# Scale's four modulation units as products on TensorE, the row norm ahead of them, the norm's copies in 256 columns

## The chip, the cores and the metric

The kernel runs on one core of a Trainium2 chip. The metric is the device time of one execution in microseconds; lower is better. Five engines work side by side and meet only at semaphores: TensorE (PE, matmuls; its weight loads are shown apart as PEld), VectorE (DVE), ScalarE (ACT), GpSimd (POOL) and SyncE (SP), which issues most of the DMAs.

## The reference

Two blocks of layers run one after the other over 256 tokens of width 1024, all in float32. The first block has two hybrid layers, the second two layers with a mixer and a mixture of experts. The change touches the beginning of the first layer of the first block:

```
mod = (c_act @ w_ada + b_ada)[:, None, :]          # 1024 -> 6 * 1024
sh1, sc1, g1, sh2, sc2, g2 = jnp.split(mod, 6, axis=-1)
h = rmsnorm(x, norm1_w) * (1 + sc1) + sh1
u = h @ w_in
```

c_act is silu(c), one row of 1024 numbers. So shift (sh1) and scale (sc1) are two vectors of 1024, each the product of one row with a 1024 x 1024 matrix, and nothing of the layer's products can start without both.

## The kernel before

The tokens are two row tiles of 128; the width is 8 chunks of 128. Each large product is made of three: weights and activations are split into a high half (fp32r, written by ScalarE as a copy) and a low half (the difference, written by VectorE), and TensorE adds high x high, high x low and low x high (`product`, L2148). Weights come in groups of 1 MB through a ring of three raw slots; SyncE loads the next group into a slot when VectorE has read it (L710, semaphores raw_read). The halves of a group lie in whi and wlo, three groups each.

The modulation is computed in units of 1 MB: unit n covers two chunks of 128 input rows for one of the six vectors. Units 0 to 3 are shift's, 4 to 7 scale's, 8 is the first unit of the gate's. Units 0 to 2 lie in the raw slots; units 3 to 8 lie in raw_deep, which is the same memory as the halves: unit 3 where the first group's high half will go, unit 6 where its low half will go (`early`, L620). SyncE issues them in the order unit 0, x, units 1 to 7, then two groups of w_in, then unit 8 and some constants (L687 to L703).

`early_ada` (L1286) is VectorE's work on one unit: for each of its two chunks, a row of 1024 is multiplied by one number per partition and added to an accumulator [128 x 1024]. After four units `sum_mod` (L2131) lets TensorE sum the accumulator over the partitions: for each of 8 column blocks one matmul with the block as stationary side and one column of ones as the moving side. `take_mod` (L1325) adds the bias columns, `norm_columns` (L1339) makes the columns by which the norm scales.

Each engine runs its instructions in the order in which the program writes them. VectorE at the start of layer 0 (L1556 to L1583): c_act, units 0 and 1, the transposed parameter columns (pcol), unit 2, the mean squares and inverse roots of the two row tiles (`mean_square`, `rsqrt`), units 3 to 7, shift and scale, norm_columns, the low half of group 0, then the norm's copies. ScalarE (L882 to L893): the squares, roots and row scaling of both tiles, the high half of group 0 once both accumulators are done (L888), the high halves of the copies, the high half of group 1. TensorE (L2204 to L2218): turns the scaled rows tile by tile (`turn_tile`), the two sums, then product 0 for row tile 0 and for row tile 1, and product 1.

The norm's copies (`modulated`, L1361) go from PSUM to the buffer ft, which has two places: four instructions of 128 columns for each of four quarters (row tile, half of the width). `high_tile` on ScalarE and `low_tile` on VectorE make the halves of a quarter. In the other places of the kernel a PSUM bank holds two chunks of 256 tokens, and `turn`, `high` and `low` handle a bank.

Of the kernel before, what the change touches and what calls it, by code (L numbers as in the profile page):

```python
# [29 lines left out]
ALU = mybir.AluOpType  # L30
# [3 lines left out]
P = 128  # L34
T = 256
D = 1024
KD = D // P
NT = T // P
# [31 lines left out]
ADA = 4  # L70
# [177 lines left out]
def program(nc, A, out):  # L248
    with ExitStack() as top:
# [27 lines left out]
        ft = sb("ft", [P, 2, 2 * T])  # L277
# [342 lines left out]
        def early(n):  # L620

            part = raw[:, n] if n < RAW else raw_deep[:, n - RAW]
            return parts_of(part, 2, D)
# [196 lines left out]
        def _(act):  # L820
# [13 lines left out]
            for l in range(LAYERS):  # L834
# [20 lines left out]
                def high_tile(f, t, h):  # L855

                    act.wait_ge(*ft_ready.at(l, ft_index(f) + 1))
                    act.activation(tile_part(xt_hi, t, h), chunks_of_tile(ft[:, f % 2, :]), ACT.Copy).then_inc(ft_hi.sem, 1)
# [23 lines left out]
                if l == 0:  # L882
                    for t in range(NT):
                        square(t)
                    for t in range(NT):
                        root(NORM1 + t, t, t + 1)
                        scale_rows(NORM1, t)
                    act.wait_ge(*acc_done.at(0, 2))  # L888
                    split(0)
                    for t in range(NT):  # L890
                        for h in range(2):
                            high_tile(X_NORM1 + 2 * t + h, t, h)
                    split(1)  # L893
                else:

                    act.wait_ge(*x_final.at(l - 1, 5))
                    square(0)
                    root(NORM1, 0, 1)
                    scale_rows(NORM1, 0)
                    split(1)  # L900
                    act.wait_ge(*x_final.at(l, 0))
                    square(1)
                    for h in range(2):
                        high_tile(X_NORM1 + h, 0, h)
                    root(NORM1 + 1, 1, 2)
                    scale_rows(NORM1, 1)
                    for h in range(2):
                        high_tile(X_NORM1 + 2 + h, 1, h)
# [289 lines left out]
        def _(dve):  # L1198
# [46 lines left out]
            for l in range(LAYERS):  # L1245
# [40 lines left out]
                def early_ada(n):  # L1286

                    vec, i = divmod(n, ADA)

                    dve.wait_ge(early_in[n], 16)  # L1290
                    if i == 0:

                        dve.wait_ge(*acc_read.at(0, vec - 1))
                    w, a = early(n), acc[:, vec % 2, :]
                    for k in range(2):
                        c = cact[:, 2 * i + k:2 * i + k + 1]
                        if i == 0 and k == 0:
                            ins = dve.tensor_scalar(a, w[:, k, :], c, None, ALU.mult)
                        else:
                            ins = dve.scalar_tensor_tensor(out=a, in0=w[:, k, :], scalar=c, in1=a, op0=ALU.mult, op1=ALU.add)  # L1300
                        if k == 0:
                            lk(ins)
                    ins.then_inc(early_read, 1)
                    dve.wait_ge(early_read, n + 1)
                    if n < RAW:
                        dve.sem_inc(raw_read[n].sem, 1)
                    if i == ADA - 1:
                        dve.sem_inc(acc_done.sem, 1)
# [16 lines left out]
                def take_mod(vec, l=l):  # L1325

                    dve.wait_ge(*acc_read.at(l, vec + 1))
                    if vec in (2, 5):
                        i = vec // 3

                        dve.wait_ge(*grow_in.at(l, 32))
                        b = MOD_BANK[vec]
                        dve.tensor_tensor(grow[:, i, :], mp[:, b:b + 2, :].rearrange("p a n -> p (a n)"), grow[:, i, :], ALU.add).then_inc(mod_taken.sem, 1)
                    else:
                        c = MOD_COL[vec]
                        src = gp[:, 0, vec, 0:KD] if l == 0 and vec < 2 else mp[:, MOD_BANK[vec], c:c + KD]
                        dve.tensor_tensor(modc[:, vec, :], src, pcol[:, l, KD * vec:KD * (vec + 1)], ALU.add).then_inc(mod_taken.sem, 1)

                def norm_columns(i, vec, l=l):  # L1339

# [215 lines left out]
                if l == 0:  # L1556
                    dve.wait_ge(csig_ready, 1)
                    lk(dve.tensor_tensor(cact[:, :], mp[:, 2, 0:KD], csig[:, :], ALU.mult))
                    early_ada(0)
                    early_ada(1)  # L1560
                    dve.wait_ge(params_t, LAYERS)
                    for i in range(LAYERS):
                        dve.tensor_copy(pcol[:, i, :], mp[:, i, 0:PC_ROWS]).then_inc(params_ready, 1)
                    dve.wait_ge(params_ready, LAYERS)
                    early_ada(2)
                    for t in range(NT):
                        mean_square(0, t)
                    for t in range(NT):
                        rsqrt(NORM1 + t, t, t + 1)
                    for n in range(3, 2 * ADA):  # L1570
                        early_ada(n)
                    take_mod(0)
                    take_mod(1)
                    norm_columns(0, 0)
                    split(0)
                    modulated(X_NORM1, 0, 0, 0, 0)
                    for t, h in ((0, 1), (1, 0), (1, 1)):
                        modulated(X_NORM1, 0, 0, t, h)
                        low_tile(X_NORM1, *((0, 0), (0, 1), (1, 0))[2 * t + h - 1])
                    low_tile(X_NORM1, 1, 1)  # L1580
                    split(1)
                    early_ada(2 * ADA)
                    dve.wait_ge(params_in, PARAMS)  # L1583
                else:
                    norm_tail(X_NORM1, 0, 0, NORM1, 0, lambda: split(1))
# [532 lines left out]
        def _(pe):  # L2118
# [25 lines left out]
                mm.then_inc(acc_read.sem, 1)  # L2144


            for l in range(LAYERS):
                def product(s, tiles=range(NT)):  # L2148

# [52 lines left out]
                    pe.wait_ge(*mod_taken.at(l, 2))  # L2202

                if l == 0:  # L2204
                    for t in range(NT):
                        pe.wait_ge(*xn_ready.at(l, t + 1))
                        turn_tile(t)
                    pe.wait_ge(zeroed, 2)
                    sum_mod(0, 0)
                    sum_mod(1, 0)  # L2210
                    pe.wait_ge(*mod_taken.at(0, 2))
                if l == 0:
                    pe.wait_ge(*ft_lo.at(l, X_NORM1 + 1))
                    product(0, (0,))
                    pe.wait_ge(*ft_lo.at(l, X_NORM1 + 3))
                    product(0, (1,))
                    pe.wait_ge(*ft_lo.at(l, X_NORM1 + 4))
                    product(1)  # L2218
                else:
                    begin(0, X_NORM1, 0)  # L2220
                poolcur = poolw[:, l, :, :]
# [492 lines left out]
```

## Time and profile before

| | |
|---|---|
| median of three runs | 1791.11 us (1787.89 to 1794.01) |
| the profiled execution's own time | 1795.38 us |
| its span | 1793.6 us |
| TensorE busy | 1581.0 us, 88% |
| VectorE busy | 938.0 us, 52% |
| ScalarE busy | 620.4 us, 35% |
| DMA | 427.65 MB, 238 GB/s in the mean |

The span is from the first to the last recorded instruction. Busy shares are means over stages with different limits; what an edit is worth is read from the waits of its own stage. In a row of a timeline the first number is the start in us, the second the time from the start of the first to the end of the last of the instructions that it merges; in brackets stands the idle time before them and what ended it.

### The profile page before, as it was taken

To read this page: it belongs to the slowest core of one execution; us is meant where nothing else is said; L and a number is where in the kernel's file an instruction comes from. 1 tells how busy PE (TensorE), PEld (TensorE's weight loads), DVE (VectorE), ACT (ScalarE), POOL (GpSimd) and SP (SyncE) were. 2 spreads that over 40 slices of the span, in tenths; PEclk is the share of its full clock that TensorE was granted. 3 is DMA by queue.
4 is the path that set the end of the run, shared out by engine and by line. 5 is a ranking of instruction groups with operands and counts; after the bars stand their busy time and mean duration, and the time that the engine had idled before them with its cause. 6 is when DMAs were issued, how large, how long until landed. Compare 5 with 4: busy or idle time off the path is not lost.

```text
span 1793.6 us, 18858 instructions
## 1 busy us (share of the span) xinstructions
PE 1581.0 (88%) x7463; PEld 1088.6 (61%) x7463; DVE 938.0 (52%) x1402; ACT 620.4 (35%) x881; POOL 49.8 (3%) x66
## 2 busy tenths in 40 slices
PE   2799988999889998899979995999996996799985
PEld 2687767888768776788868874333334875433331
DVE  4897667765478666764556665110006675311102
ACT  2354444433345444443425651111114472111111
POOL 2000000000000000000020200000000010000000
PEclk9999999999989998999989897999998998899998
DMA  9576534876466543575646425999994516599994
GB/s 338 197 236 213 185 119 168 307 244 242 164 216 241 200 164 128 172 235 169 219 128 204 129 83 200 377 409 409 409 400 144 167 48 247 200 409 409 409 409 190
DMA packets 149963, 427.65 MB, mean 238 GB/s; under 512 B 8104, under 2 KB 16544, under 8 KB 149872
## 3 DMA queue, kind: packets, MB, share of 16 engines
q1 hardware_dynamic: 146192, 417.43, 63.6%
q0 software_dynamic: 3456, 8.87, 1.8%
q8 instruction: 64, 1.05, 0.2%
q14 instruction: 27, 0.22, 0.0%
q10 hardware_dynamic: 224, 0.07, 0.0%
HBM read 425.30 MB, written 1.05 MB: 238 GB/s over the span
## 4 chain that ended last, share of the span: by engine, by line
PE 43%; DVE 7%; SPq 6%; DMA 3%; issue 1%; ACT 1%; DVEq 0%
PE gp L2164 11%; PE gp L2553 9%; PE gp L2372 9%; SPq L734 6%; PE gp L2572 4%; PE mp L2593 2%; DMA raw_more<-in_exp_w_up 2%; PE gp L2538 2%; PE mp L2427 1%; PE mp L2426 1%; PE mp L2391 1%; DVE stats L1706 1%; PE mp L2415 1%; PE mp L2435 1%; DMA raw<-in_w_in 1%
## 5 line engine op out<-in xcount | busy, mean ns | idle before, releaser
L1315 DVE TENSOR_TENSOR wlo<-raw,whi 128x2048 fp32r<-128x2048 f32 (+1 forms) x132 | 289.5, 2194 | 206.5 <-ACT whi L842 205.2
L2164 PE MATMUL gp<-whi,xt_hi 128*128 128x512 f32 (+1 forms) x800 | 320.1, 400 | 31.9 <-DVE xt_lo L1376 20.5
L842 ACT ACTIVATE whi<-raw 128x2048 fp32r<-128x2048 f32 (+1 forms) x132 | 242.2, 1835 | 300.0 <-PE gp L2164 188.1
L2164 PE MATMUL gp<-wlo,xt_hi 128*128 128x512 f32 (+1 forms) x800 | 312.9, 391 | 0.0
L2164 PE MATMUL gp<-whi,xt_lo 128*128 128x512 f32 (+1 forms) x800 | 312.5, 391 | 0.0
L2164 PEld LDWEIGHTS gp<-whi,xt_hi 128*128 128x128 f32 x800 | 155.4, 194 | 72.2 <-DVE xt_lo L1376 15.9
L2164 PEld LDWEIGHTS gp<-whi,xt_lo 128*128 128x128 f32 x800 | 155.4, 194 | 31.4
L2164 PEld LDWEIGHTS gp<-wlo,xt_hi 128*128 128x128 f32 x800 | 155.7, 195 | 30.0 <-issue 1.0
L2031 DVE TENSOR_SCALAR pr<-slots,key,dg 128x128 f32<-128x128 f32 x64 | 19.3, 344 | 260.5 <-PE gp L2583 260.5
L2372 PE MATMUL gp<-whi,xt_hi 128*128 128x512 f32 (+1 forms) x224 | 86.2, 385 | 6.0 <-DVE xt_lo L1751 3.1
L1225 DVE SCALAR_TENSOR_TENSOR acc<-raw,cact,acc 128x1024 f32<-128x1024 f32 x69 | 88.5, 1282 | 2.5 <-DMA raw<-in_w_ada 1.1
L2045 DVE TENSOR_TENSOR pr<-pr,gp 64x512 f32<-64x512 f32 x32 | 21.7, 679 | 123.2 <-ACT pr L1145 123.2
L2372 PE MATMUL gp<-whi,xt_lo 128*128 128x512 f32 (+1 forms) x224 | 84.6, 378 | 0.0
L2372 PE MATMUL gp<-wlo,xt_hi 128*128 128x512 f32 (+1 forms) x224 | 84.6, 378 | 0.0
L1242 DVE TENSOR_TENSOR wlo<-raw,whi 128x2048 fp32r<-128x2048 f32 (+3 forms) x32 | 59.5, 1859 | 34.1 <-ACT whi L1018 32.8
L1139 ACT ACTIVATE cgc<-gp 128x256 f32<-128x256 f32 x32 | 12.3, 384 | 185.7 <-PE gp L2583 185.7
L2164 PE MATMUL gp<-whi,at_hi 128*128 128x512 f32 x176 | 69.9, 397 | 4.3 <-DVE at_lo L1414 4.3
L2164 PE MATMUL gp<-wlo,at_hi 128*128 128x512 f32 x176 | 69.2, 393 | 0.0
L2164 PE MATMUL gp<-whi,at_lo 128*128 128x512 f32 x176 | 69.1, 392 | 0.0
L2572 PE MATMUL gp<-raw_deep,pr 128*64 128x512 f32 x288 | 65.4, 596 | 1.5 <-ACT pr L1140 1.5
L2553 PE MATMUL gp<-raw_deep,xg_second 128*64 128x512 f32 x256 | 61.6, 626 | 5.7 <-DMA raw_deep<-in_exp_w_up 5.7
L1018 ACT ACTIVATE whi<-raw 128x2048 fp32r<-128x2048 f32 (+3 forms) x36 | 57.4, 1601 | 25.4 <-PE gp L2372 13.4
(390 smaller groups left out, 2356.0 us busy)
## 6 DMA issues: line engine op xcount, KB each, us to landing
raw<-in_w_in SPq DMA_DIRECT2D x60, 1024.0 KB, 5.5
raw<-in_w_ada SPq DMA_DIRECT2D x42, 1024.0 KB, 5.5
raw_deep<-in_exp_w_down SPq DMA_DIRECT2D x36, 1024.0 KB, 16.9
raw_deep<-in_exp_w_gate SPq DMA_DIRECT2D x30, 1024.0 KB, 14.4
raw_deep<-in_exp_w_up SPq DMA_DIRECT2D x30, 1024.0 KB, 16.8
raw<-in_w_gate SPq DMA_DIRECT2D x20, 1024.0 KB, 5.1
raw<-in_w_up SPq DMA_DIRECT2D x20, 1024.0 KB, 5.1
raw<-in_w_down SPq DMA_DIRECT2D x20, 1024.0 KB, 5.0
```

The source lines that it names most:

```text
L734: sp.dma_start(parts_of(part, units, cols), src).then_inc(there.sem, 16)
L842: act.activation(slot(whi, s % SPLIT, units, cols), slot(raw, g % RAW, units, cols), ACT.Copy).then_inc(hi_done.sem, 1)
L1018: act.activation(slot(whi, s % SPLIT, units, cols), parts_of(part, units, cols), ACT.Copy).then_inc(hi_done.sem, 1)
L1225: ins = dve.scalar_tensor_tensor(out=a, in0=w[:, k, :], scalar=c, in1=a, op0=ALU.mult, op1=ALU.add)
L1242: dve.tensor_tensor(slot(wlo, s % SPLIT, units, cols), parts_of(part, units, cols), slot(whi, s % SPLIT, units, cols).bitcast(F32), ALU.su ...
L1315: dve.tensor_tensor(slot(wlo, s % SPLIT, units, cols), slot(raw, g % RAW, units, cols), slot(whi, s % SPLIT, units, cols).bitcast(F32), AL ...
L2164: mm = pe.matmul(gp[:, q % 2, t, 0:wide], a[:, chunk, ts], w[:, unit, c0:c0 + wide], start=first and n == 0 and m == 0, stop=last and n == ...
L2372: mm = pe.matmul(gp[:, q % 2, t, 0:cols], a[:, chunk0 + unit, ts], w[:, unit, :], start=first and unit == 0 and m == 0, stop=last and unit ...
L2538: mm = pe.matmul(bank, h[:, t, P * c:P * (c + 1)], pick[:, t, :], start=t == 0 and h is h_hi, stop=t == 1 and h is h_lo)
L2553: mm = pe.matmul(bank[columns, :], a[:, chunk0 + c, column0:column0 + CAP], w[:, c, :], start=first and c == 0, stop=last and c == 3)
L2572: mm = pe.matmul(bank_y[CAP * n:CAP * (n + 1), :], ag[:, CAP * chunk:CAP * (chunk + 1)], w[:, c, COLS * n:COLS * (n + 1)], start=chunk == ...
L2593: mm = pe.matmul(mp[:, 2 * t + half, :], back[rows, P * t:P * (t + 1)], yx[rows, :], start=e == 0, stop=e == NE - 1)
```

## The change

Four things change, all in layer 0 of the first block.

1. VectorE takes units 0 to 3 only, and the parameter columns and both row norms come right behind unit 0, ahead of unit 1.
2. Units 4 to 7 become matmuls on TensorE (`unit_product`): a 128 x 128 block of the unit is the stationary side, the chunk's column of c_act the moving side, and the results add up in 8 columns of a PSUM bank, which start from scale's bias columns by a product with the identity. VectorE then copies these columns instead of adding the bias. TensorE sums the shift's accumulator ahead of the last unit. ScalarE's first split waits for TensorE's last unit (acc_read) instead of VectorE's (acc_done), because it overwrites what TensorE reads.
3. TensorE turns both row tiles together, bank by bank, and products 0 and 1 are each made for both tiles at once.
4. The norm's copies are made bank by bank, two instructions of 256 columns each, in an order in which two banks go ahead of VectorE's first split.

```diff
@@ ScalarE
-                    act.wait_ge(*acc_done.at(0, 2))
+                    act.wait_ge(*acc_read.at(0, 2))
                     split(0)
-                    for t in range(NT):
-                        for h in range(2):
-                            high_tile(X_NORM1 + 2 * t + h, t, h)
+                    for b in range(4):
+                        high(X_NORM1 + b, xt_hi[:, 2 * b:2 * b + 2, :])
                     split(1)
@@ early_ada
-                    dve.wait_ge(early_read, n + 1)
+                    dve.wait_ge(early_read, n + 1 if n < ADA else n + 1 - ADA)
@@ take_mod
-                        dve.tensor_tensor(modc[:, vec, :], src, pcol[:, l, KD * vec:KD * (vec + 1)], ALU.add).then_inc(mod_taken.sem, 1)
+                        if l == 0 and vec == 1:
+                            dve.tensor_copy(modc[:, vec, :], src).then_inc(mod_taken.sem, 1)
+                        else:
+                            dve.tensor_tensor(modc[:, vec, :], src, pcol[:, l, KD * vec:KD * (vec + 1)], ALU.add).then_inc(mod_taken.sem, 1)
@@ VectorE, layer 0
                     early_ada(0)
-                    early_ada(1)
                     dve.wait_ge(params_t, LAYERS)
                     for i in range(LAYERS):
                         dve.tensor_copy(pcol[:, i, :], mp[:, i, 0:PC_ROWS]).then_inc(params_ready, 1)
                     dve.wait_ge(params_ready, LAYERS)
-                    early_ada(2)
                     for t in range(NT):
                         mean_square(0, t)
                     for t in range(NT):
                         rsqrt(NORM1 + t, t, t + 1)
-                    for n in range(3, 2 * ADA):
+                    for n in range(1, ADA):
                         early_ada(n)
                     take_mod(0)
                     take_mod(1)
                     norm_columns(0, 0)
+
+                    def normed(b):
+                        f = X_NORM1 + b
+                        bank_done(f)
+                        for k in range(2):
+                            c = 2 * b + k
+                            ins = dve.tensor_scalar(ft[:, f % 2, T * k:T * (k + 1)], mp[:, b, T * k:T * (k + 1)],
+                                                    scol[:, 0, c:c + 1], modc[:, 0, c:c + 1], ALU.mult, ALU.add)
+                            if k == 0:
+                                lk(ins)
+                        ins.then_inc(ft_ready.sem, 1)
+
+                    def low_bank(b):
+                        low(X_NORM1 + b, xt_hi[:, 2 * b:2 * b + 2, :], xt_lo[:, 2 * b:2 * b + 2, :])
+
+                    normed(0)
+                    normed(1)
+                    low_bank(0)
                     split(0)
-                    modulated(X_NORM1, 0, 0, 0, 0)
-                    for t, h in ((0, 1), (1, 0), (1, 1)):
-                        modulated(X_NORM1, 0, 0, t, h)
-                        low_tile(X_NORM1, *((0, 0), (0, 1), (1, 0))[2 * t + h - 1])
-                    low_tile(X_NORM1, 1, 1)
+                    low_bank(1)
+                    normed(2)
+                    normed(3)
+                    low_bank(2)
+                    low_bank(3)
                     split(1)
                     early_ada(2 * ADA)
@@ TensorE
+            def unit_product(vec, i):
+
+                pe.wait_ge(early_in[ADA * vec + i], 16)
+                w = early(ADA * vec + i)
+                if i == 0:
+
+                    pe.matmul(gp[:, 0, vec, 0:KD], ident[:, :], pcol[:, 0, KD * vec:KD * (vec + 1)], start=True, stop=False)
+                for k in range(2):
+                    j = 2 * i + k
+                    for c in range(KD):
+                        mm = pe.matmul(gp[:, 0, vec, c:c + 1], w[:, k, P * c:P * (c + 1)], cact[:, j:j + 1],
+                                       start=False, stop=j == KD - 1 and c == KD - 1)
+                if i == ADA - 1:
+                    mm.then_inc(acc_read.sem, 1)
@@ TensorE, layer 0
-                    for t in range(NT):
-                        pe.wait_ge(*xn_ready.at(l, t + 1))
-                        turn_tile(t)
+                    pe.wait_ge(*xn_ready.at(l, 2))
+                    for b in range(4):
+                        turn(b, xn2, 2 * P * b).then_inc(tr_done.sem, 1)
                     pe.wait_ge(zeroed, 2)
-                    sum_mod(0, 0)
-                    sum_mod(1, 0)
+                    for i in range(ADA):
+                        if i == ADA - 1:
+                            sum_mod(0, 0)
+                        unit_product(1, i)
+                    pe.sem_inc(acc_done.sem, 1)
                     pe.wait_ge(*mod_taken.at(0, 2))
                 if l == 0:
-                    pe.wait_ge(*ft_lo.at(l, X_NORM1 + 1))
-                    product(0, (0,))
-                    pe.wait_ge(*ft_lo.at(l, X_NORM1 + 3))
-                    product(0, (1,))
-                    pe.wait_ge(*ft_lo.at(l, X_NORM1 + 4))
-                    product(1)
+                    for s in range(2):
+                        pe.wait_ge(*ft_lo.at(l, X_NORM1 + 2 * s + 2))
+                        product(s)
```

## Rows read from the trace of the kernel before

**Rows 1.** The page: the span and TensorE's busy time, share and instructions.
```profile
span 1793.6 us, 18858 instructions
PE 1581.0 (88%) x7463; PEld 1088.6 (61%) x7463; DVE 938.0 (52%) x1402; ACT 620.4 (35%) x881; POOL 49.8 (3%) x66
```

**Rows 2.** Timeline of SyncE's queue: the issues of units 4 and 7.
```profile
4.98 0.50 SPq L685 DMA_DIRECT2D raw_deep<-in_w_ada  x1
...
13.34 7.05 SPq L685 DMA_DIRECT2D raw_deep<-in_w_ada  x1
```

**Rows 3.** DMA issues: the same two, KB, then us from issue to landing.
```profile
raw_deep<-in_w_ada SPq DMA_DIRECT2D x1, 1024.0 KB, 24.4
...
raw_deep<-in_w_ada SPq DMA_DIRECT2D x1, 1024.0 KB, 23.8
```

**Rows 4.** Timeline of all engines, 14 to 31 us: units and row norm.
```profile
14.36 1.28 ACT L863 ACT_TABLE_LOAD   x1
...
19.25 2.60 DVE L1300 SCALAR_TENSOR_TENSOR acc<-raw,cact,acc 128x1024 f32<-128x1024 f32 x2 [9.42 <-DMA raw<-in_w_ada]
...
27.62 1.15 ACT L871 ACTIVATE xn<-x,rr 128x1024 f32<-128x1024 f32 x1 [1.00 <-DVE rr L1354]
...
28.91 1.94 PE L2173 MATMUL mp<-ident,xn 128*128 128x128 f32 x8 [16.04 <-ACT xn L871]
```

**Rows 5.** Timeline of all engines, 32 to 46.3 us: the two sums over partitions.
```profile
32.82 3.41 PE L2143 MATMUL gp<-ones,acc 128*128 128x1 f32 x16
...
42.65 1.91 ACT L842 ACTIVATE whi<-raw 128x2048 fp32r<-128x2048 f32 x1 [11.64 <-DVEq L1308]
...
42.67 3.57 PE L2143 MATMUL gp<-ones,acc 128*128 128x1 f32 x16 [6.43 <-DVEq L1308]
...
46.28 0.17 DVE L1337 TENSOR_TENSOR modc<-gp,pcol 128x8 f32<-128x8 f32 x1 [3.41 <-PE gp L2143]
```

**Rows 6.** Timeline of all engines, 48 to 77 us: copies, splits, first products.
```profile
48.89 3.40 DVE L1366 TENSOR_SCALAR ft<-mp,scol,modc 128x128 f32<-128x128 f32 x8
50.67 0.63 ACT L858 ACTIVATE xt_hi<-ft 128x512 fp32r<-128x512 f32 x1 [6.11 <-DVE ft L1366]
52.21 0.68 DVE L1376 TENSOR_TENSOR xt_lo<-ft,xt_hi 128x512 fp32r<-128x512 f32 x1
...
52.99 0.76 PE L2164 MATMUL gp<-whi,xt_hi 128*128 128x512 f32 x1 [6.75 <-DVE xt_lo L1376]
...
59.71 2.29 DVE L1315 TENSOR_TENSOR wlo<-raw,whi 128x2048 fp32r<-128x2048 f32 x1 [1.11 <-ACT whi L842]
...
62.15 0.47 PE L2164 MATMUL gp<-whi,xt_hi 128*128 128x512 f32 x1 [0.86 <-DVE wlo L1315]
...
74.05 2.28 DVE L1315 TENSOR_TENSOR wlo<-raw,whi 128x2048 fp32r<-128x2048 f32 x1
76.25 1.28 DVE L1225 SCALAR_TENSOR_TENSOR acc<-raw,cact,acc 128x1024 f32<-128x1024 f32 x1
```

**Rows 7.** Line 2143, the sums: ns min/median/max, first and last start.
```profile
L2143 PEld LDWEIGHTS mp<-ones,acc x96: 188/192/338, 213.5 to 662.9; 128*128 128x128 f32 x96
...
L2143 PEld LDWEIGHTS gp<-ones,acc x32: 287/333/337, 32.6 to 45.8; 128*128 128x128 f32 x32
L2143 PE MATMUL gp<-ones,acc x32: 213/352/372, 32.8 to 45.9; 128*128 128x1 f32 x32
```

**Rows 8.** Stretches: length, busy us and instructions by engine, granted clock, DMA share, GB/s.
```profile
213.60:215.60 2.00, 2.00 (x21) 2.00 (x20) 1.93 (x4) 0.00 (x0) 0.00 (x0) 0.99 1.05 390
215.60:218.40 2.80, 2.80 (x15) 2.80 (x15) 0.06 (x1) 0.00 (x0) 0.00 (x0) 0.50 0.98 333
53.00:58.60 5.60, 5.60 (x13) 4.38 (x14) 5.17 (x11) 1.99 (x3) 0.00 (x0) 1.00 0.07 28
58.60:61.30 2.70, 2.68 (x12) 1.88 (x10) 1.59 (x1) 2.70 (x2) 0.00 (x0) 1.00 0.00 0
```

**Rows 9.** Line 1623: a copy of 256 columns from PSUM, ns min/median/max.
```profile
L1623 DVE TENSOR_SCALAR ft<-mp,pcol x4: 483/484/486, 220.7 to 665.9; 128x256 f32<-128x256 f32 x4
```

**Rows 10.** SyncE's waits from 62 us on: total us, times, longest.
```profile
SPq L693 <- DVE wlo L1315: 690.9, 124, 19.4
SPq L734 <- DVE wlo L1242: 268.3, 32, 48.2
```

## The prediction

> **What bounds the kernel now.** I read the page's first part, then the start of the run as a timeline, then the DMA issues, then the waits behind the start. TensorE is busy 88% of the span [rows 1], so most of the run is a chain of products on TensorE, fed by splits that ScalarE and VectorE make. The page's chain of waits is followed back only to 675 us, so the stage that changes has to be read from the timeline.
>
> At the start the chain is this. SyncE issues the loads of eight modulation units in a row, 0 to 3 for shift and 4 to 7 for scale. They land one behind the other: unit 4 at 4.98 + 24.4 = 29.4 us, unit 7 at 13.34 + 23.8 = 37.1 us [rows 2, 3]. VectorE takes them one at a time, 2.60 us for two accumulations [rows 4], and is done with unit 7 at about 42.6. TensorE then sums the second accumulator over the partitions: 16 matmuls in 3.57 us, to 46.24 [rows 5]. VectorE forms the columns, splits the first weights, writes the norm's copies, and the first product starts at 52.99 [rows 6]. From there VectorE is the one that ends last: the second split starts at 59.71, then a leftover unit, a split, another unit and the rotary angles follow without a gap to the split of 74.05 [rows 6]; TensorE waits for it. So what counts is how much the VectorE operation of 59.71 moves. The path to it is: columns known (46.24), plus 13.47 us.
>
> **Part 1, row norm ahead.** The parameter columns and the two row norms go ahead of unit 1. ScalarE's squares are ready at 14.3 and its table for the root is loaded from 14.36 for 1.28 us [rows 4], so the first root comes at 15.7, the five short VectorE steps after it end at 16.8, ScalarE's scaling of 1.15 us [rows 4] ends at 18.0, the second root and steps end at 19.1 and the second scaling at 20.2. VectorE is free at 19.1, just before unit 1 lands (it starts on it at 19.25 now [rows 4]), so this costs nothing there: the DMA's landing hides it. The turns of both row tiles, 8 in 1.94 us [rows 4], take 16 x 0.24 = 3.9 us and end at 24.2 instead of 33.0. Nothing waited for them before 46.68, so this gains nothing by itself: it moves them out of TensorE's way, which now has other work from 29.4 on.
>
> **Part 2, VectorE's half.** Units 4 to 7 leave VectorE: 4 x 2 accumulations, some 10.1 us. The landings are (37.1 - 29.4) / 3 = 2.6 us apart, so unit 3 lands at about 26.8 and VectorE has finished it at 29.5. From then VectorE idles until the columns come. The loads behind it are not touched: the two raw slots are released by units 0 and 1, at the same times as before.
>
> **Part 3, TensorE's half, the term that decides.** One unit is 2 chunks x 8 columns = 16 matmuls with a 128x128 block of weights in f32 as the stationary side and a single moving column. The trace has this operation: the sum over partitions is 8 such matmuls, and appears as 16 instructions with 16 weight loads [rows 5, 7]. So each matmul is two instructions. Sixteen of them took 3.57 us with the last one lasting 0.35 [rows 7], hence (3.57 - 0.35) / 15 = 0.2147 us from one to the next. It is the weight load that is paid, for a single column, and there is no saving from having only one column. Counted out: 2 for the bias columns (identity by parameter columns), 4 x 32 = 128 for the units, and 16 for the first accumulator's sum, which stands between units 6 and 7. Together 146 instructions x 0.2147 = 31.35 us. They start when unit 4 lands, at 29.45 us, and no later unit is late: one lands every 2.6 us and takes 6.9 us to multiply. The last ends at 29.45 + 31.35 + 0.14 (the tail of the last one) = 60.95 us. In the kernel before the same point was 46.24: 14.7 us later. VectorE needed 2.60 us for a unit, TensorE needs 6.9.
>
> Why the slow price: the loads of these sums last 333 ns at the start and 192 ns in the median later on [rows 7]. In the later place the first 2 us held 21 instructions at a granted clock of 0.99, and the next 2.8 us held 15 at 0.50 [rows 8]; so the engine had its 2.4 GHz level from the dense products before, and fell to 1.2 GHz in the middle of a run of one-column matmuls, which did not keep it. At the start the printed clock is 1.00, but the spacing of the first dense products says 1.2 GHz: 13 of 512 columns in 5.6 us, then 12 in 2.7 us [rows 8]. They rose only after 5.6 us of dense work; the 7.5 us of turns and sums before (28.9 to 36.4) had not raised it, since the sum at 42.67 is still at 0.21 [rows 5]. From both sides: the price is 0.107 where the engine stays at full clock (half of 0.2147, and about the 21 in 2 us), and 0.333 if no load overlaps the matmul before it. I take 0.2147: same shape, same level, same DMA load (the first sum ran while the queues were full).
>
> The Trainium skill, "TensorE: Matmul & The Clock Gate", section "LDWEIGHTS (loading the stationary operand)", gives a load as the column count over 1.2 GHz, 107 ns for 128 columns, whatever the rows. By that rule 146 loads would be an estimated 15.6 us and TensorE would nearly keep up with the landings; the row's 0.215 is twice it, and the measurement decides the sum.
>
> **Part 4, behind the columns.** Call E the end of the last unit's product. ScalarE waited for the accumulators before (42.65) and splits the first weights beside TensorE's second sum [rows 5]; now its buffer is free only at E, because the units lie where the halves go. Split from E to E + 1.9 [rows 5], and the high copy behind it. VectorE: copy of the scale columns and the norm columns to E + 0.44; two copies of 256 columns, 4 x 0.484 [rows 9], to E + 2.4. The high copy of bank 0 ends at E + 2.55 (0.63 each), the low one (0.68 [rows 6]) at E + 3.25, the split (2.29) at E + 5.5, the second low at E + 6.15. The first product starts at E + 6.2 = 67.2, against 52.99. Copies 2 and 3 end at E + 8.15, their lows at E + 9.6; ScalarE's second split begins at E + 8.8 behind its last high copy and takes 1.9, so VectorE's second split starts at E + 10.8. Before it was 13.47 behind: 16 copies of 128 columns, 8 of them in 3.40 us [rows 6], have become 8 of 0.484, and the tile-wise order with its waits has gone. This part gives back 2.7 us. Product 0, now in one piece, runs from 67.2 at the low level first: 5.6 + 11 x 0.226 = 8.1 us, to 75.3; product 1 follows to 80.8 and product 2 to 86.3.
>
> **The sum.** VectorE's second split: 60.95 + 10.8 = 71.75 against 59.71, so +12.0 us. Behind it VectorE's row is the same and unbroken, so the split of 74.05 moves to 86.1 and ends at 88.4, after product 2 (86.3): VectorE still ends last there, and all of the 12.0 goes on. The loads of the following slots start when VectorE has read a slot (SyncE's longest wait is that one, 690.9 us in 124 times [rows 10]), so the transfers move by the same amount and nothing runs ahead of it. Own time 1795.38 (span 1793.6) + 12.0 = 1807.4. The runs' median is 1791.11, 4.3 us below the profiled one, so the forecast is 1791.1 + 12.0 = 1803.1 us.
>
> **The rivals.**
> A, the other side: a unit costs TensorE half. For it: at the full level the same matmul goes at 0.107 [rows 8]. The place is the run from 29.45; the units would take 3.4 us each and E comes at 29.45 + 146 x 0.107 = 45.1, which is 1.1 before today's; with Part 4 the second split starts at 55.9, 3.8 us earlier: 1787.3, faster. It decides below a price of 0.13: E + 10.8 equals 59.71 at E = 48.9, which leaves 19.3 us for 146 instructions. Against it: three runs of this shape show the low level. The Trainium skill's rule on the weight load, above, would end here too.
> B, slower at the start but given back later: 1791 to 1794. For it: SyncE waits a lot, and a later stage that was bound by transfers could hide the delay. Against: the wait of SyncE is for VectorE's reads, so no transfer runs ahead [rows 10]; the mechanism needs a load that starts by itself.
> C, dearer: the loads don't overlap, since here each brings a new 1 MB of weights that a transfer has just written: 146 x 0.333 = 48.6, E = 78.1, +29.2: 1820. Against: the same matmul overlapped at the start with the queues full.
> D, the clock rises part of the way: after some of the 31 us of steady work TensorE gets 2.4 GHz. Half the run at 0.107 gives E = 53, +4 us: 1795. For it: the longest unbroken run of such matmuls in [rows 8] is 4.8 us, and 31 us of them are not shown. Against: those fell, none rose.
>
> **How the numbers follow.** The forecast has 0.77, A 0.07, B 0.05, C 0.04, D 0.07. A kernel like this can't be told from no change within 0.3%, 5.4 us. Faster: A less a part of its noise, 0.07. Same: B, most of D: 0.08. Slower: 0.85. The range: the forecast's own is 1803 plus or minus 5 (the three runs before lie 6 us apart, and the terms of Part 4 are good to 1 us); down to D it is 1797, up 1809. That leaves out A, B and C, 0.16 with the edges.
>
> **What would show it.** In the profile after: a unit's 32 instructions in about 6.9 us; loads of 333 ns; the last unit's end at 61; ScalarE's first split at 61 instead of 42.65; the first product at 67; VectorE's second split at 71.8; DVE idle from 29.5 to 54. Units with loads of 0.19 would prove A or D; a first product at 67 and a span under 1800 would prove B.

## The result, and the profile after

| | before | after |
|---|---|---|
| median of six runs | 1793.83 us | 1805.45 us (1803.1 to 1809.11) |
| profiled execution, span | 1793.6 us | 1807.3 us |

The ratio is 1.0069, with a 95% interval of 1.0053 to 1.0085: slower by 9.5 to 15.3 us, clear of what a measurement can tell from no change. The forecast was +12.0 us. The forecast's level, 1803.1, is 2.3 below the measured one. It was added to a median of the kernel before over three runs, 1791.11; over six runs that median is 1793.83, 2.7 higher, so the difference is the better test of the two.

The page after: span, then busy time, share and instructions by engine; it answers to [rows 1]. TensorE has 114 instructions more (130 for the units and the bias, 16 fewer for the sum that is gone) and is busy 27 us longer; VectorE is busy 12 us less.

```profile
span 1807.3 us, 19064 instructions
PE 1608.1 (89%) x7577; PEld 1114.4 (62%) x7577; DVE 926.0 (51%) x1386; ACT 620.3 (34%) x881; POOL 49.7 (3%) x66
```

The changed stage as a timeline, all engines (start us, us, engine, line, operation; in brackets the idle time before and what ended it), answering to [rows 4 to 6]. "Turns" are the 128 x 128 transposes of the scaled rows, "the columns" are shift and scale laid out over the partitions:

```profile
20.87 3.65 PE L2228 MATMUL mp<-ident,xn 128*128 128x128 f32 x16 [7.89 <-ACT xn L871]
...
26.96 2.61 DVE L1299 SCALAR_TENSOR_TENSOR acc<-raw_deep,cact,acc 128x1024 f32<-128x1024 f32 x2 [1.02 <-DMA raw_deep<-in_w_ada]
...
29.62 0.57 PE L2171 MATMUL gp<-pcol,ident 128*128 128x8 f32 x2 [5.11 <-DMA raw_deep<-in_w_ada]
...
30.04 20.62 PE L2175 MATMUL gp<-cact,raw_deep 128*128 128x1 f32 x96
...
50.52 3.55 PE L2161 MATMUL gp<-ones,acc 128*128 128x1 f32 x16
...
53.94 6.97 PE L2175 MATMUL gp<-cact,raw_deep 128*128 128x1 f32 x32
54.11 0.17 DVE L1339 TENSOR_TENSOR modc<-gp,pcol 128x8 f32<-128x8 f32 x1 [24.55 <-PE gp L2161]
60.94 0.17 DVE L1337 COPY modc<-gp 128x8 f32<-128x8 f32 x1 [6.66 <-PE gp L2175]
60.94 1.91 ACT L842 ACTIVATE whi<-raw 128x2048 fp32r<-128x2048 f32 x1 [40.21 <-PE gp L2175]
...
67.00 0.76 PE L2197 MATMUL gp<-whi,xt_hi 128*128 128x512 f32 x1 [6.10 <-DVE xt_lo L1398]
...
71.46 2.29 DVE L1314 TENSOR_TENSOR wlo<-raw,whi 128x2048 fp32r<-128x2048 f32 x1 [1.11 <-ACT whi L842]
...
85.79 2.28 DVE L1314 TENSOR_TENSOR wlo<-raw,whi 128x2048 fp32r<-128x2048 f32 x1
...
88.13 0.50 PE L2197 MATMUL gp<-whi,xt_hi 128*128 128x512 f32 x1 [2.02 <-DVE wlo L1314]
```

The reader is to see three things. TensorE is busy from 29.62 to 60.91, 31.28 of the 31.30 us in the stretch below. VectorE stands idle for 24.55 and then 6.66 us, waiting for it, and ScalarE for 40.21. And the second split starts at 71.46, where it started at 59.71: 11.75 us later, and the split of 74.05 [rows 6], that of weight group 3, at 85.79: 11.74 later; nothing was given back on the way.

The units' instructions (ns min/median/max, first and last start), then three stretches with their length, busy us and instructions by engine, granted clock, DMA share and GB/s: the whole stretch, and two pieces of 6.9 us, about a unit each. An instruction that overlaps an edge of a stretch is counted in it.

```profile
L2175 PEld LDWEIGHTS gp<-cact,raw_deep x128: 333/333/333, 30.0 to 60.5; 128*128 128x128 f32 x128
L2175 PE MATMUL gp<-cact,raw_deep x128: 352/352/352, 30.0 to 60.5; 128*128 128x1 f32 x128
```

```profile
29.60:60.90 31.30, 31.28 (x146) 31.21 (x146) 0.17 (x1) 0.00 (x0) 0.00 (x0) 0.50 0.53 198
...
36.40:43.30 6.90, 6.90 (x34) 6.90 (x34) 0.00 (x0) 0.00 (x0) 0.00 (x0) 0.50 1.05 390
...
53.70:60.60 6.90, 6.90 (x34) 6.90 (x34) 0.17 (x1) 0.00 (x0) 0.00 (x0) 0.50 0.00 0
```

146 instructions in 31.3 us at a granted clock of 0.50, the 1.2 GHz level: 0.2145 each. The count is the same, 34 in 6.9 us, with the transfers at 390 GB/s and with none at all, so the transfers don't set this price. Here the clock column says the level itself; at the start of the kernel before it printed 1.00, and only the spacing and the loads of 333 ns showed the level [rows 7, 8].

### The profile page after: what moved, and what is told of

Same layout as the page of the kernel before. It is cut to its first block, busy times and chain, and to the rows that moved or that the text cites. A ratio compares the mean times of both kernels' runs of the same rounds, so it can differ in the third digit from the quotient of the medians.

```text
span 1807.3 us, 19064 instructions
## 1 busy us (share of the span) xinstructions
PE 1608.1 (89%) x7577; PEld 1114.4 (62%) x7577; DVE 926.0 (51%) x1386; ACT 620.3 (34%) x881; POOL 49.7 (3%) x66
## 4 chain that ended last, share of the span: by engine, by line
PE 43%; DVE 7%; SPq 6%; DMA 3%; issue 1%; ACT 1%; DVEq 0%
PE gp L2197 11%; PE gp L2586 9%; PE gp L2405 9%; SPq L734 6%; PE gp L2605 4%; PE mp L2626 2%; DMA raw_more<-in_exp_w_up 2%; PE gp L2571 2%; PE mp L2460 1%; PE mp L2459 1%; PE mp L2424 1%; DVE stats L1724 1%; PE mp L2468 1%; PE mp L2448 1%; DMA raw<-in_w_in 1%
## 5 line engine op out<-in xcount | busy, mean ns | idle before, releaser
L2197 PEld LDWEIGHTS gp<-whi,xt_lo 128*128 128x128 f32 x800 | 154.8, 193 | 31.3
L2197 PEld LDWEIGHTS gp<-wlo,xt_hi 128*128 128x128 f32 x800 | 155.4, 194 | 29.8 <-issue 1.0
```

Source lines behind the costliest of these rows:

```text
L2197: mm = pe.matmul(gp[:, q % 2, t, 0:wide], a[:, chunk, ts], w[:, unit, c0:c0 + wide], start=first and n == 0 and m == 0, stop=last and n == ...
```

## The experiments

**All units back on VectorE** (norm ahead and wide copies stay; the addition of scale's bias and the semaphores go back with the units, which the diff below leaves out).

```diff
-                    for n in range(1, ADA):
+                    for n in range(1, 2 * ADA):
                         early_ada(n)
...
-                    for i in range(ADA):
-                        if i == ADA - 1:
-                            sum_mod(0, 0)
-                        unit_product(1, i)
-                    pe.sem_inc(acc_done.sem, 1)
+                    sum_mod(0, 0)
+                    sum_mod(1, 0)
```

> The changed kernel with one part undone: all eight units go back to VectorE (row norm ahead and copies in 256 columns stay). My theory: the 146 one-column instructions on TensorE are the whole loss, and the other two parts gain. VectorE follows the landings and ends unit 7 at 37.1 + 2.7 = 39.9 us, TensorE's sum takes 3.5, so the columns come at 43.5; the second split 10.6 us behind, at 54.1 instead of 59.7: 5.6 us faster than the kernel before, ratio 0.997. Rival: the new order of VectorE and ScalarE behind the columns costs something of its own (ScalarE's first split now delays the high copies, product 0 waits for both tiles): then the second split would come at 59 or later and the kernel would be no faster than before.

Measured: ratio 0.9973 (0.9957 to 0.9989), 4.8 us faster than before (2.0 to 7.7). The timeline of this kernel:

```profile
41.24 3.57 PE L2158 MATMUL gp<-ones,acc 128*128 128x1 f32 x16 [6.84 <-DVEq L1307]
...
44.85 0.17 DVE L1336 TENSOR_TENSOR modc<-gp,pcol 128x8 f32<-128x8 f32 x1 [3.41 <-PE gp L2158]
...
55.42 2.29 DVE L1314 TENSOR_TENSOR wlo<-raw,whi 128x2048 fp32r<-128x2048 f32 x1 [1.11 <-ACT whi L842]
...
69.75 2.29 DVE L1314 TENSOR_TENSOR wlo<-raw,whi 128x2048 fp32r<-128x2048 f32 x1
```

The columns come at 44.85, 1.3 later than expected because the transfers of this execution landed later (VectorE's unit 2 starts at 24.72, in the changed kernel at 23.33); from the columns to the second split it is 10.6, as expected. The split of group 3 is at 69.75, 4.3 earlier than before. The rival, a cost of the new order of its own, would have put the second split at 59 or later; it is at 55.42. So everything in the change but TensorE's units is a gain when taken together, and the units alone turn -4.8 into +12.

**The norm ahead alone**, on the kernel before.

```diff
                     early_ada(0)
-                    early_ada(1)
...
-                    early_ada(2)
...
-                    for n in range(3, 2 * ADA):
+                    for n in range(1, 2 * ADA):
```

> The kernel before with the parameter columns and both row norms ahead of unit 1, nothing else. My theory: VectorE no longer loses the 2.7 us of norm and roots between unit 2 and unit 3, and is bound by the last landing: end of unit 7 at 39.9 instead of 42.6, everything behind it 2.7 us earlier. Rival: unit 7 lands later than I read, so VectorE waits for it and gains under 1 us.

Measured: the columns at 43.48 instead of 46.28, the second split at 56.91 instead of 59.71, both 2.8 earlier (2.7 expected), so the rival is out. The whole time's ratio is 0.999 (0.9971 to 1.001): the place is shown, the gain in the whole is too small for these runs.

**The wide copies alone**, on the kernel before. The diff below shows the turns and the start of VectorE's new order; ScalarE's high halves and products 0 and 1 change as in the changed kernel.

```diff
-                    for t in range(NT):
-                        pe.wait_ge(*xn_ready.at(l, t + 1))
-                        turn_tile(t)
+                    pe.wait_ge(*xn_ready.at(l, 2))
+                    for b in range(4):
+                        turn(b, xn2, 2 * P * b).then_inc(tr_done.sem, 1)
...
-                    split(0)
-                    modulated(X_NORM1, 0, 0, 0, 0)
+                    normed(0)
+                    normed(1)
+                    low_bank(0)
+                    split(0)
```

> The kernel before with the norm's copies made bank by bank in 256 columns, both tiles turned together and products 0 and 1 for both tiles at once, nothing else. My theory: the second split comes 10.6 us behind the columns instead of 13.5, so 2.9 us faster; product 0 starts later behind the columns, which costs nothing, because VectorE ends last at the split of group 3. Rival: the later product 0 is what counts (it starts 5.9 us behind the columns, and 6.75 before, but ends later than before in relation to the second split), and the gain is under 1 us.

Measured: the second split at 56.87, the split of group 3 at 71.21, both 2.8 earlier than before (2.9 expected). The ratio of the whole is 1.0001 (0.9985 to 1.0018), which holds -2.7 us only at its edge; that the 2.8 us reach the end is not shown by this run. This kernel's timeline also shows something that the prediction had not reckoned with:

```profile
31.17 3.65 PE L2227 MATMUL mp<-ident,xn 128*128 128x128 f32 x16 [18.30 <-ACT xn L871]
34.61 2.23 PE L2160 MATMUL gp<-ones,acc 128*128 128x1 f32 x16
42.69 3.58 PE L2160 MATMUL gp<-ones,acc 128*128 128x1 f32 x16 [5.86 <-DVEq L1307]
```

The first sum behind the 16 turns took 2.23 us, the second 3.58. In the first, the loads go from 333 ns to 192 at about 35.3, some 4 us behind the first turn: the level came up within the sum. It was down again at 38.8, where the clock column goes from 1.00 to 0.50, 2 us after TensorE had run out of work.

**Half of each unit's products.**

```diff
-                for k in range(2):
+                for k in range(1, 2):
                     j = 2 * i + k
```

> The changed kernel with only the second chunk of each of scale's four units multiplied (the first chunk's 8 matmuls are left out, so scale is incomplete). 64 instructions less. My theory, a price of 0.2147 us each in a row that is bound by TensorE: the last unit ends at 47.2 instead of 60.9, the second split at 58.0; 13.7 us faster than the changed kernel and 1.7 us faster than before. Rival: TensorE waits for landings or fetches at the start of each unit, a fixed price per unit: then halving the count saves clearly less, under 8 us.

The rest of this kernel isn't comparable: with other numbers one of the two layers of the second block takes its branch in which every expert is computed for every token, and the whole takes 2377 us. Only its start is read here:

```profile
29.98 0.56 PE L2171 MATMUL gp<-pcol,ident 128*128 128x8 f32 x2 [5.43 <-DMA raw_deep<-in_w_ada]
30.40 10.38 PE L2175 MATMUL gp<-cact,raw_deep 128*128 128x1 f32 x48
40.64 3.55 PE L2161 MATMUL gp<-ones,acc 128*128 128x1 f32 x16
44.05 3.55 PE L2175 MATMUL gp<-cact,raw_deep 128*128 128x1 f32 x16
```

From 29.98 to 47.60 it is 17.6 us; in the changed kernel it is 31.3 from 29.62. 64 instructions less, 13.7 us less, 0.214 each: the price is per instruction, and a fixed price per unit is ruled out. The columns are at 47.64 and the second split at 58.17 (58.0 expected).

**Dense work ahead of the units.** The products write a PSUM bank that nothing reads.

```diff
+                    pe.wait_ge(x_in, 16)
+                    pe.wait_ge(zeroed, 2)
+                    for _ in range(4):
+                        pe.matmul(gp[:, 1, 0, :], ones[:, :], x[:, 0, 0:COLS], start=True, stop=True)
                     pe.wait_ge(*xn_ready.at(l, 2))
                     for b in range(4):
                         turn(b, xn2, 2 * P * b).then_inc(tr_done.sem, 1)
-                    pe.wait_ge(zeroed, 2)
+                    for _ in range(6):
+                        pe.matmul(gp[:, 1, 0, :], ones[:, :], x[:, 0, 0:COLS], start=True, stop=True)
```

> The changed kernel with work on TensorE that nothing reads, ahead of the units: 4 products of 512 columns in f32 between the transposed parameters and the turns of the norm, and 6 more between the turns and unit 4. The theory that the price of a one-column matmul follows the granted clock: the first instructions of unit 4 go at 0.107 us with loads of 192 ns, until the level falls some us later as in [rows 8], and from there at 0.215; each us at the full level moves the last unit's end 1 us forward, so it comes 2 to 6 us earlier than 60.9 and the kernel is 8 +- 2 us slower than before instead of 12. Rival: the price is the weight's way out of memory, whatever the clock: 0.215 from the first one on and the time of the changed kernel. If the level has not risen by the turns, the six products last twice as long, and unit 4 starts late by some 5 us.

Stretches of this kernel, unit 4 from 29.8 on, then the units' loads (ns min/median/max):

```profile
30.50:31.50 1.00, 1.00 (x11) 1.00 (x10) 0.00 (x0) 0.00 (x0) 0.00 (x0) 1.00 1.02 406
31.50:32.50 1.00, 1.00 (x8) 1.00 (x8) 0.00 (x0) 0.00 (x0) 0.00 (x0) 0.72 1.01 395
32.50:33.50 1.00, 1.00 (x6) 1.00 (x6) 0.00 (x0) 0.00 (x0) 0.00 (x0) 0.50 1.05 406
...
L2175 PEld LDWEIGHTS gp<-cact,raw_deep x128: 192/333/338, 29.7 to 58.3; 128*128 128x128 f32 x128
```

The same instruction on the same data: 11 in a us at the full level, 6 in a us at half of it (with those that overlap the edges), with the transfers at 406 GB/s both times. Without the edges, 20 of them started between 29.77 and 31.90, some 0.11 us apart. The loads take 192 ns at the one level and 333 at the other. So the price follows the level, and the rival is out. The last unit ends at 58.7 and the second split is at 69.24, 2.2 earlier than in the changed kernel, the lower end of what I expected. The whole time's ratio is 1.0063 (1.0045 to 1.0082), 11.3 us slower than before (8.1 to 14.7) where I had expected 8 +- 2; it can't be told from the changed kernel's.

**The same, with one dense product ahead of each half unit**, against the kernel of the last experiment.

```diff
                     j = 2 * i + k
+                    pe.matmul(gp[:, 1, 0, :], ones[:, :], x[:, 0, 0:COLS], start=True, stop=True)
                     for c in range(KD):
```

> The same with one more such product of 512 columns (two instructions, 0.43 us each at the full level) ahead of each half unit. If that keeps the level: 146 x 0.107 + 16 x 0.43 = 22.5 us from 29.5, the last unit ends at 52, 9 us earlier than in the changed kernel, and the kernel is 3 us slower than before. If the level falls all the same: 31.35 + 16 x 0.85 = 45 us, the last unit ends at 74.5 and the kernel is 25 us slower than before.

Timeline of TensorE in this kernel:

```profile
30.55 2.10 PE L2176 MATMUL gp<-cact,raw_deep 128*128 128x1 f32 x16
32.50 2.06 PE L2174 MATMUL gp<-x,ones 128*128 128x512 f32 x2
34.35 3.41 PE L2176 MATMUL gp<-cact,raw_deep 128*128 128x1 f32 x16
```

The second branch came true: ratio 1.0134 (1.0118 to 1.0151), 24 us slower than before, and the columns at 71.9, 2.6 before the 74.5 that I had for the last unit. The first half unit took 2.10 us: it ran at the full level until 32.0, 1.4 us into it, and the level fell there. All the others took 3.41. One product of 512 columns for every 8 of one column neither kept the level nor brought it back.

**One unit on TensorE, the others on VectorE**, against the version with all units on VectorE.

```diff
                     for n in range(1, 2 * ADA):
-                        early_ada(n)
+                        if n != ADA:
+                            early_ada(n)
...
                     sum_mod(0, 0)
+                    unit_product(1, 0)
                     sum_mod(1, 0)
```

(The sum over partitions then adds to unit 4's columns instead of starting them.)

> Row norm ahead and copies in 256 columns as in the changed kernel, but only unit 4 on TensorE, units 5 to 7 on VectorE with the sum over partitions behind them. TensorE has unit 4 done at 36.5 (7.1 us from its landing), well ahead of unit 7's landing at 37.1. My theory, VectorE is bound by the last landing once the norm is ahead: the same as with all units on VectorE, the columns at 43.5 or up to 0.5 us earlier, 5 us faster than before. Rival: any unit taken off VectorE's row saves its 2.6 us, columns at 41.

VectorE's units 5 to 7 and TensorE's last sum in this kernel:

```profile
31.53 0.75 DVE L1297 TENSOR_SCALAR acc<-raw_deep,cact 128x1024 f32<-128x1024 f32 x1 [2.51 <-DMA raw_deep<-in_w_ada]
...
34.16 5.25 DVE L1299 SCALAR_TENSOR_TENSOR acc<-raw_deep,cact,acc 128x1024 f32<-128x1024 f32 x4 [0.56 <-DMA raw_deep<-in_w_ada]
...
39.88 3.55 PE L2162 MATMUL gp<-ones,acc 128*128 128x1 f32 x16
```

Measured: ratio 0.9968 (0.9956 to 0.9981), 5.7 us faster than before; the columns at 43.47 and the second split at 53.99. The columns are where my theory has them with all units on VectorE (43.5), and 2.5 later than by the rival. TensorE did the first sum before unit 4 and so had it done only at 40.0, 0.6 after VectorE's last accumulation (39.41); the time of the columns alone therefore doesn't tell the theory from the rival. VectorE's own row does: the time that it was spared became waiting for the landings of units 5 and 6, 2.51 and 0.56 us, and it ended at 39.41 all the same, 2.7 behind the last landing. Relief of VectorE by a unit is worth nothing here, because the last landing sets the end.

**All units on VectorE, with two splits moved:** norm ahead, wide copies, and the splits of groups 0 and 1 moved into the idle time around the last sum. The diff is against the version with all units on VectorE.

```diff
@@ ScalarE
                     split(0)
+                    split(1)
                     for b in range(4):
                         high(X_NORM1 + b, xt_hi[:, 2 * b:2 * b + 2, :])
-                    split(1)
@@ VectorE
                     take_mod(0)
+                    split(0)
                     take_mod(1)
...
                     low_bank(0)
-                    split(0)
                     low_bank(1)
```

> All units on VectorE, row norm ahead, copies in 256 columns, and the splits of groups 0 and 1 moved into the idle time around the last sum over partitions: ScalarE makes both high halves right behind the accumulators (39.9 to 43.8), VectorE the low half of group 0 while TensorE sums (41.9 to 44.2, 0.7 past the columns). Theory: the second split leaves its wait for ScalarE (1.1) and the path loses 2.3 - 0.7: it starts at 51.4, 8.3 us earlier than before and 2.7 us earlier than with all units on VectorE alone; the kernel 8 us faster than before, ratio 0.9955. Rival: the load of group 3, issued when the second split is done, lands 5.7 us later and ScalarE's split of it ends last, or TensorE is the one that ends last at the split of group 3 (product 0 starts at the low level): then under 6 us.

VectorE's timeline in this kernel:

```profile
41.63 2.29 DVE L1314 TENSOR_TENSOR wlo<-raw,whi 128x2048 fp32r<-128x2048 f32 x1 [1.72 <-ACT whi L842]
43.84 0.16 DVE L1336 TENSOR_TENSOR modc<-gp,pcol 128x8 f32<-128x8 f32 x1
...
51.16 2.29 DVE L1314 TENSOR_TENSOR wlo<-raw,whi 128x2048 fp32r<-128x2048 f32 x1
...
65.50 2.28 DVE L1314 TENSOR_TENSOR wlo<-raw,whi 128x2048 fp32r<-128x2048 f32 x1
```

Measured: ratio 0.9963 (0.9949 to 0.9977), 6.6 us faster than before (4.1 to 9.1, with 8 expected), so it is faster than both the kernel before and the changed one. The second split is at 51.16 (51.4 expected), without its wait for ScalarE, and the split of group 3 at 65.50, 8.55 earlier than before. TensorE still waits for that split, 0.77 us, so the rival is out for this place. In the whole time this version can't be told from the one without the moved splits (0.9973), only in the trace.

## Why the prediction was right, by its own steps

| step | predicted | measured |
|---|---|---|
| VectorE done with unit 3 | 29.5 | 29.57 |
| first matmul of the units | 29.45 | 29.62 |
| price of an instruction | 0.2147 | 0.2145 |
| last unit ends | 60.95 | 60.91 |
| first product | 67.2 | 67.00 |
| second split | 71.75 | 71.46 |
| split of group 3 | 86.1 | 85.79 |
| TensorE's wait for it | 2.1 | 2.02 |
| the whole | +12.0 | +12.4 (+9.5 to +15.3) |

*Part 1* held: the turns ended at 24.5 (24.2), since x landed 0.5 us later. VectorE came to unit 1 at 19.46, 0.2 later than before, and its wait for unit 2's landing (1.27 us) took that up. The experiment with the norm ahead alone shows what this part would be worth in the kernel before, 2.8 us on VectorE's row; in the changed kernel nothing of it reached the end, since TensorE was the one to wait for.

*Part 3* held to the instruction. It was right because a row with the same shape was there, and because its instructions were counted as the trace counts them, two for a matmul in f32, rather than as the program writes them. The half units isolate the price, 0.214 us per instruction, and the one unit agrees (34 instructions in 7.4 us); the return to VectorE isolates what the whole part costs: without it the change is 4.8 us faster than before.

The Trainium skill, "TensorE: Matmul & The Clock Gate", section "LDWEIGHTS (loading the stationary operand)", has 107 ns for a load of 128 columns. The runs show that spacing only at the full level (some 0.11 us between starts in the fifth experiment); at the lower one it is 215 ns, and the estimate of 15.6 us for the 146 loads was half of the 31.3 measured. "Nearly keep up" was too strong even by that rule: 32 loads of 107 ns are an estimated 3.4 us for a unit, against one landing every 2.6.

*Part 4* gave back 2.9 us, not 2.7: from the last unit's end to the second split it took 10.55 us (10.8). A wide copy took 0.54 us; the 0.484 came from the row of a copy that has one operand per partition, where this one has two. That cost 0.2 us for four copies. Against it, nearly every instruction started about 0.1 us before the recorded end of the one ahead of it on its engine, which the sum had left out. Two small errors of opposite sign made this part come out so close.

*The rivals.* A (half the price) had the right condition, the level, and the wrong size for how long it could last: even with TensorE brought to the full level on purpose, it fell some 2 us into the units. C (no overlap of loads) is refuted by the spacing. D (the level rises in the 31 us) is refuted by the stretch at 0.50. The range's lower end was set too high for D: it was to reach down to D, but D's own number, 1795, lies below 1797.

B (given back later) is refuted at the split of group 3, where the delay is still 11.74 of 11.75, and by the whole time. The argument against it misread one row: 690.9 us is SyncE's largest total of waits, not its longest wait [rows 10]. The experiments are the better ground. Wherever the split of group 3 moved, the whole moved by about as much:

| kernel | split of group 3, us against 74.05 | whole time, us against before |
|---|---|---|
| changed | +11.7 | +12.4 (+9.5 to +15.3) |
| dense work ahead | +9.5 | +11.3 (+8.1 to +14.7) |
| dense work ahead of half units too | +22.7 | +24.0 (+21.2 to +27.1) |
| norm ahead alone | -2.8 | -1.8 (-5.2 to +1.8) |
| wide copies alone | -2.8 | +0.2 (-2.7 to +3.2) |
| all units on VectorE | -4.3 | -4.8 (-7.7 to -2.0) |
| one unit on TensorE | -5.7 | -5.7 (-7.9 to -3.4) |
| splits moved too | -8.6 | -6.6 (-9.1 to -4.1) |

The wide copies alone are the one row that lies at the edge of its interval, or just outside; why their 2.8 us don't show in the whole stays open.

One argument was weaker than I put it, and here the forecast had some luck. I wrote that turns and sums had not raised the level, because the sum at 42.67 was slow, and took it as ground for the low price. That sum can't tell: in the kernel with the wide copies the first sum ended at the full level, and the second, 5.86 us later, was as slow. With the half units, the last three of the 16 turns took 404 to 273 ns instead of 421, so turns alone can raise the level. In the changed kernel itself the clock column goes from 1.00 to 0.50 at 28.1. So the level had been up before; when it rose isn't recorded, and it can only have been at the end of the turns or just behind, since all 16 took 421 ns or more. It fell during the 5.11 us in which TensorE waited for unit 4, 1.5 us before the units began. It isn't the same in every kernel: with one unit on TensorE and with the splits moved, the same 16 turns are followed by no such fall, and by a slow sum. So the units started at the low level because TensorE had idled ahead of them, and they stayed there because 31 us of one-column matmuls didn't raise it. That such a run doesn't hold the level either I had from [rows 8]; the rise and the fall ahead of it I had not seen. Had the units begun at the full level, by the fifth experiment that would have been worth about 2 us, not the 16 of rival A.

## What to carry to other kernels

Before work goes from one engine to another because it idles, compare the two engines' time for a piece with the rate at which the pieces arrive: VectorE's 2.6 us per MB kept up with the transfers' 2.6 us, TensorE's 6.9 could not. A product of a matrix with one vector pays a weight load for every 128 x 128 block of the matrix, and in f32 two of them (8 matmuls are 16 instructions). With 8 moving columns, in the two instructions for the bias, the spacing was the same 0.21 us as with one. And a long run of such products went at the lower clock. When the last landing sets the end, relief of the engine behind it is worth nothing; what pays is to move work out of the path behind that landing, as the trace of the two moved splits showed.

## What the runs showed of the hardware

- One-column matmuls don't hold TensorE's clock: after dense products at 1.00 the level fell to 0.50 1.4 to 2.2 us into them, although the engine was never idle (at 215.6 and 659.3 us in the kernel before, at 32.0 in both kernels with dense work ahead), and one product of 512 columns for every 8 of one column did not prevent it.
- The clock column can print 1.00 where the engine runs at the lower level, at the start of the run before its first change: the sum at 42.7 printed 1.00 in the kernel before and 0.50 in the one with the wide copies, with 3.57 and 3.58 us. Weight loads of 333 ns against 192 tell the level.
- The start of an execution varies by the landings: unit 2 was taken at 22.9 to 24.7 us in these profiles, which is as much as some of the effects. Distances within a profile were steadier than positions: from the columns to the second split 10.5 to 10.6 us in the kernels with wide copies and the old order of splits.
